# Down phase of an fp32 MLP kernel: four groups of products three uses apart instead of two, with later splits and loads at the phase edges

## What is computed

```python
h = h + rmsnorm(mix, post_mix_gain[l])
v = rmsnorm(h, pre_mlp_gain[l])
ff = jnp.square(jax.nn.relu(jnp.einsum("bsd,df->bsf", v, mlp_w_up[l].astype(v.dtype))))
ff = jnp.einsum("bsf,fd->bsd", ff, mlp_w_down[l].astype(v.dtype))
h = h + rmsnorm(ff, post_mlp_gain[l])
```

## Time and profile before

| | |
|---|---|
| median of 3 runs | 2196.18 us (2189.27 to 2198.07) |
| profiled execution, own time | 2191.95 us |
| its span, first to last instruction | 2188.8 us |
| TensorE busy | 97% |
| VectorE, ScalarE, GpSimd busy | 65%, 48%, 11% |
| mean granted TensorE clock | 0.992 of full speed |
| DMA, mean over the span | 182 GB/s |

### The profile page before, as it was taken

The page is one execution under the profiler, slowest core; times in us unless marked ns, Lnnn a source line. Parts: engine busy times, 40 slices in busy tenths (PEclk is TensorE's granted clock), DMA queues, the critical chain, the costliest instruction groups (busy, mean ns, idle before and its releaser), DMA issues.

```text
span 2188.8 us, 28875 instructions
## 1 busy us (share of the span) xinstructions
PE 2120.9 (97%) x9781; PEld 1743.9 (80%) x9781; DVE 1425.9 (65%) x2309; ACT 1049.8 (48%) x1821; POOL 237.0 (11%) x228
## 2 busy tenths in 40 slices
PE   8999999999999999989999899999899999999996
PEld 6777788888888788778888688888787888888885
DVE  4877666666666646776666766666576666666666
ACT  5564545555555534555555665555332333333333
POOL 6001000000001000033200000000333310000001
PEclk9999999999999999999999999999999999999999
DMA  7246644644544726578755865554877755444467
GB/s 262 109 152 207 205 154 135 201 146 145 196 150 144 259 87 199 154 232 275 254 152 151 272 178 145 144 142 130 308 240 242 264 187 163 135 154 135 143 151 168
DMA packets 317493, 397.82 MB, mean 182 GB/s; under 512 B 15296, under 2 KB 204256, under 8 KB 317392
## 3 DMA queue, kind: packets, MB, share of 16 engines
q1 hardware_dynamic: 295728, 317.46, 46.0%
q0 software_dynamic: 19360, 70.72, 10.3%
q10 hardware_dynamic: 2304, 8.39, 0.9%
HBM read 262.09 MB, written 134.41 MB: 181 GB/s over the span
## 4 chain that ended last, share of the span: by engine, by line
PE 81%; DVE 3%; DMA 2%; ACT 2%; issue 1%; SPq 0%; ACTq 0%; DVEq 0%; POOLq 0%
PE o_ps L1847 20%; PE o_ps L1849 19%; PE o_ps L1848 19%; PE m_unit_ps L516 18%; DMA o_s_lo<-ff_d 1%; PE o_ps L1878 1%; PE m_nd_ps L577 0%; PE m_bank L565 0%; PE m_nd_ps L576 0%; PE m_s_ps L556 0%; PE m_nd_ps L528 0%; PE m_nd_ps L529 0%; PE m_nd_ps L585 0%; DVE o_acc L2461 0%; DMA o_b_lo<-v_d 0%
## 5 line engine op out<-in xcount | busy, mean ns | idle before, releaser
L516 PE MATMUL m_unit_ps<-u_hi,w_hi 128*128 128x512 f32 x768 | 309.1, 402 | 1.4 <-ACT floor L796 1.1
L516 PE MATMUL m_unit_ps<-u_hi,w_lo 128*128 128x512 f32 x768 | 300.8, 392 | 0.0
L516 PE MATMUL m_unit_ps<-u_lo,w_hi 128*128 128x512 f32 x768 | 299.7, 390 | 0.0
L1847 PE MATMUL o_ps<-w_hi,o_s_hi 128*128 128x512 f32 x704 | 274.9, 391 | 7.0 <-ACT o_stage_c L2039 5.6
L1849 PE MATMUL o_ps<-w_hi,o_s_lo 128*128 128x512 f32 x704 | 274.0, 389 | 0.0
L1848 PE MATMUL o_ps<-w_lo,o_s_hi 128*128 128x512 f32 x704 | 273.9, 389 | 0.0
L2482 DVE TENSOR_TENSOR o_acc<-o_ps,o_acc 128x512 f32<-128x512 f32 x256 | 172.0, 687 | 148.8 <-PE o_ps L1849 148.7
L2071 ACT ACTIVATE o_s_hi<-o_s_lo 128x512 fp32r<-128x512 f32 x129 | 81.1, 631 | 270.7 <-DMA o_s_lo<-ff_d 270.2
L516 PEld LDWEIGHTS m_unit_ps<-u_hi,w_lo 128*128 128x128 f32 x768 | 144.5, 188 | 32.0
L516 PEld LDWEIGHTS m_unit_ps<-u_hi,w_hi 128*128 128x128 f32 x768 | 144.9, 189 | 29.7 <-issue 1.9
L516 PEld LDWEIGHTS m_unit_ps<-u_lo,w_hi 128*128 128x128 f32 x768 | 145.1, 189 | 27.6
(11 more groups left out here) (383 smaller groups left out, 4474.0 us busy)
## 6 DMA issues: line engine op xcount, KB each, us to landing
o_s_lo<-ff_d SPq DMA_DIRECT2D x129, 256.0 KB, 2.8
o_up_raw<-in_mlp_w_up SPq DMA_DIRECT2D x32, 1024.0 KB, 5.9
ff_d<-o_stage_c SPq DMA_DIRECT2D x128, 256.0 KB, 5.8
u_hi<-uhi_d SPq DMA_DIRECT2D x12, 2048.0 KB, 10.7
u_lo<-ulo_d SPq DMA_DIRECT2D x12, 2048.0 KB, 15.1
ff_d<-o_stage_s SPq DMA_DIRECT2D x96, 256.0 KB, 5.6
o_a_lo<-ff_d SPq DMA_DIRECT2D x95, 256.0 KB, 2.7
w_raw<-in_w_in POOLq DMA_DIRECT2D x24, 512.0 KB, 5.5
```

The lines of the kernel that those rows point to most:

```text
L516: last = nc.tensor.matmul(unit_bank[u][:], w[u][:, c, :], x[:, b, c, :], start=(c == 0 and z == 0), stop=(c == KT - 1 and z == 2))
L1847: nc.tensor.matmul(dst, sh, mh, start=(begins and i == 0), stop=False, skip_group_check=not begins)
```

## The change

Six edits. The groups of the down phase stand three uses apart, not two, so that the phase has 41 sets in place of 38 and the first sets hold only group 0 (three sets, six products), then groups 0 and 1. The idle slots s4 and a12 take products a11 and s2 of use 2, and s3 takes a12 of use 29. The split of each new form is placed no later than two steps ahead of its first use. The first chunk's forms are loaded later (at steps 0, 4, 7, 18 and not 0, 1, 3, 10), as are their splits, the stores of set 31 and the last gain vector. At the turn, form 2 is loaded ahead of the stores of set 14 and is split at the end of set 15, and forms 3 to 6 are split one place later each. GpSimd starts its slab sums when the left operands of set 3 are made, where it started when the first forms were.

```diff
-        sets = [[(p, s - 2 * DOWN[p][1]) for p in DOWN if 0 <= s - 2 * DOWN[p][1] < self.USES]
-                for s in range(self.USES + 6)]
+        sets = [[(p, s - 3 * DOWN[p][1]) for p in DOWN if 0 <= s - 3 * DOWN[p][1] < self.USES]
+                for s in range(self.USES + 9)]
...
-        other = {("a11", 1): "s3", ("s2", 1): "a22", ("a12", self.USES - 2): "a11", ("a12", self.USES - 1): "s2"}
+        other = {("a11", 1): "s3", ("s2", 1): "a22", ("a12", self.USES - 3): "s3", ("a12", self.USES - 2): "a11", ("a12", self.USES - 1): "s2"}
+        other |= {("a11", 2): "s4", ("s2", 2): "a12"}
...
-            self.low_at.append(-1 if m < 4 else max(min(self.high_at[m] + 2, m - 3), self.low_at[-1]))
+            self.low_at.append(-1 if m < 4 else max(min(self.high_at[m] + 2, m - 3), self.high_at[m], self.low_at[-1]))
...
-        rest = [(3, ("s4", 0)), (6, ("s3", 0)), (9, ("a22", 0)), (16, ("a12", 0))]
-        rest += [(self.index[p, 8 * c - 1] + 4, (p, c)) for c in range(1, 4) for p in DOWN]
+        rest = [(3, ("s4", 0)), (9, ("s3", 0)), (12, ("a22", 0)), (24, ("a12", 0))]
+        rest += [(min(self.index[p, 8 * c - 1] + 4, self.index[p, 8 * c] - 2), (p, c)) for c in range(1, 4) for p in DOWN]
...
# SP, up_set
+                if is_set(S, PAIRS - 1):
+                    load_form(2)
                 if not is_set(S, 0) and not is_set(S, SETS - 1):
                     store_ff(S - 1, 1 - b, 0 if is_set(S, PAIRS) else B)
                 if is_set(S, PAIRS - 1):
-                    for i in range(2, 7):
+                    for i in range(3, 7):
                         load_form(i)
...
# SP, down steps
-                if m in (0, 1, 3, 10):
-                    load_down({0: "s4", 1: "s3", 3: "a22", 10: "a12"}[m], 0)
-                if 5 <= m <= 8:
+                if m in (0, 4, 7, 18):
+                    load_down({0: "s4", 4: "s3", 7: "a22", 18: "a12"}[m], 0)
+                if 9 <= m <= 12:
...
# POOL
-            pool.wait_ge(*form_lo_made.at(14))
+            pool.wait_ge(*slot_lo_made.at(4 * 7))
...
# ScalarE, up_set (VectorE alike): turn is set 15, turned set 16
-                        second_form(4)
+                        second_form(3)
...
-                        second_form(5)
+                        second_form(4)
...
+                if turned:
+                    second_form(5)
...
-                if turn:
-                    second_form(2)
...
-                if turn:
-                    second_form(3)
...
+                if turn:
+                    second_form(2)
```

14 lines of the change are left out of this document (7 added, 7 removed).

## The result

| | before | after |
|---|---|---|
| median of 5 runs | 2194.13 us (2189.27 to 2198.07) | 2207.52 us (2204.70 to 2210.74) |
| profiled execution, own time and span | 2191.95, 2188.8 us | 2207.26, 2204.4 us |
| ratio | | 1.0075, 95% interval 1.0058 to 1.0093 |

The forecast was 2195.4 us (2183.5 to 2205.0), no measurable change, with a chance of 0.10 for slower. The median lies above that range.

A forecast was written before the change was run, and what follows sets the result against it. TensorE was taken as the bound, with only its pauses to win. Terms −3.8 − 3.4 + 0.3 + 1.0 + 1.6 + 1.5 + 2.0 = −0.8 gave 2191.15 us profiled; the median, 4.2 higher, 2195.4 (2183.5 to 2205).

The forecast's parts named there:

- the first steps: Start of the down phase: m = 5 waits for the copy of m = 4, pause about 6.5 us; +0.3 us.
- the tail: m = 214 to 221: operand loads have three products behind the one freeing their slot, before four; +2.0 us.
- GpSimd's start: Up phase: slab sums from set 3 remove TensorE's pauses in sets 1 and 2; −3.8 us, bounds −3.8 and 0.
- the turn: Sets 15 and 16: s4 of set 15 no longer waits for form 2, but a pause remains in set 16; −3.4 us.
- changes of a form: Three forms wanted one product earlier, at m = 30, 33 (+1.6 us) and 204 (+1.5 us).
- m = 7 to 30: Opening of the down phase: operand loads have four products behind the one freeing their slot, before six; +1.0 us.
- The slower rival: Opening and tail: operand loads land late and stall products, two pauses lower the clock; 2208 us, chance 0.12.
- three signs: Wrong if m = 5 starts within 3 us of its turn, set 16 has no pause, or opening landings average over 8 us.

The follow-up runs named there:

- later forms a step earlier: The changed kernel with each later form split at least three steps ahead of its first use, not two: 2199.49 us, 1.0040 of the kernel before.
- three repairs: The changed kernel with s4's first form split at step 4, s3's and a22's at 18 and 21, later forms three steps ahead: 2199.34 us, 1.0050 of before.

## Why the prediction was wrong

**Right: what bounds the kernel, the up phase, the first steps, the tail.** GpSimd's start and the turn were priced at −3.8 and −3.4 and gave −7.0 together, −2.8 and −4.1 in the pair of traces; each has a kernel of its own with a measured gain. That the sum came out this close is in part luck, since traces of one and the same up phase differ by almost 5 us in the start of m = 0. The first steps, +0.3, gave +0.4, with the wait where it was put. The tail, +2.0, gave +1.6.

**Wrong: the term "changes of a form", +1.6 and +1.5, which came to +7.1 and +6.5.** The prediction had the right places and the right wait, and named pauses of 1.4 to 3 us there; they were 2.4, 3.9 and 4.7. What it sized wrong was each pause.
- The chain. "Each is 2.72 − 1.3 = 1.4 late" took the quiet case's 6.67 us from an operand's load to the end of the form's split. It took 8.3 us for m = 30 (VectorE behind with other work) and 9.5 us for m = 33 (a split of 4.08 us beside GpSimd's additions for the 2.36 us that were taken for all, and a landing of 3.8). The allowance of 2.2 for a busier queue was too small for both.
- The raw form at m = 204. Its chain was counted from the operand alone, like the others. But a12 of chunk 3 has five products between its old values' last use and its first new one, two fewer than before, and the form landed only at 2123.6, 0.5 us before m = 204 should have started. That was to be read in the order. At most 1.8 us of the 4.66 are the operands that ScalarE took first (2123.6 to 2125.39).
- The clock. The sum counted a slow product behind the pause at m = 5, and none behind these three. After pauses of 2.42, 3.94 and 4.66 us the next product took 4.20, 4.41 and 4.41 us, 4.9 us over the stride in all. The earlier trace rows made this look safe: behind 2.60 us at m = 41 the next product came on time.

These sizes vary. In the five kernels that keep this order and these later splits, m = 30 starts 2.0 to 5.1 us over its stride and m = 33 1.1 to 4.7; m = 204 always 4.7 to 4.8. The last is the distance; the other two depend on when operands land and on whether the split falls beside GpSimd's additions.

What the experiments show of the cause: two apart, with all else changed, the same three forms (first used at m = 38, 41 and 196) start 2.2, 0 and 0 us over the stride. Three apart with the splits three steps ahead, m = 33 comes on time in both kernels that have it (later forms a step earlier, three repairs), m = 30 still waits, and m = 204 keeps 4 us. With seven products everywhere, m = 204's pause is gone, and in chunk 1 what is left follows GpSimd's additions (at m = 32 1.0 us over the stride in one kernel, 3.4 in the other, with the split at 2.36 and 4.51 us). So at m = 204 it is the distance, and at m = 30 and 33 mostly the split's step and length. How much the operands' extra product adds there, no kernel took apart.

**Wrong: the term "m = 7 to 30", +1.0, which came to +7.5 up to m = 18 alone.** The prediction named the split of s3 at step 9 ahead of the add that m = 12 waits for (m = 12 waited 1.2 us) but priced operand loads. The split of a22 at step 12 stands likewise ahead of the copy that m = 16 waits for, and it was left out: 3.78 us and 1.56 for the slow product. In the trace of before these two splits took 2.35 us each, and m = 7 to 18 lost 0.7 in all. The order has 12 products in sets of four now (m = 6 to 17), where the second product of a group follows two behind the first; it had 8.

**The slower rival gave the right time mostly for a wrong reason.** It put 2208 on operand loads that land late and stop the product that needs them, and 2207.5 was measured. TensorE waited for operands' low parts only 2.0 us in all (the line L2345 above), and landings of operands between 1549 and 1600 us had a median of 3.6 us, less than before (5.6). But a late operand does its harm another way: ScalarE takes it ahead of a form, so the form's split comes late. ScalarE sat idle for one 5.67 us before m = 16, 4.92 us before m = 33 and 6.45 us before m = 204, and two of these loads took 8.0 and 8.1 us to land. Outside the first steps no term priced a late operand on this path.

**The range** was too narrow at the top because the upper bounds of the form terms, +5 and +3, held no slow product and no slower split, and because I treated the terms' ends as independent: one mechanism, less time for a form, raised three of them together. None of the three signs that the prediction named for being wrong showed: they watched the first steps, the turn and the mean landing, and the loss was elsewhere.

The Trainium skill, "SBUF — State Buffer", section "🔬 SBUF: two separate sides", has GpSimd and a VectorE operation with two SBUF inputs exclude each other. The traces agree: a form split takes 2.36 us alone and 3.4 to 4.6 beside GpSimd's additions. I drew on it for the up phase, where TensorE gained from moving the additions all the same, and not for the form splits, where it cost time.

What stays open: which of the opening's loads, stores and splits frees m = 7 to 18, and what the operands' distance adds at the form changes of chunk 1.

## What to carry to other kernels

When an order is stretched, count for every shared buffer the products between its last old use and its first new one, at the edges too, where sets are smaller. A change of one or two there takes slack that the steady middle never shows. Count the steps from a split to its first use as well, and look at what stands ahead of it on its engine: a load of something else that lands late delays it too. Put a long operation of the engine that frees the accumulators where nothing waits behind it, and not between two products of one accumulator. Price each new pause with a slow restart as a chance, and each split at its length beside the engine that stretches it.

## What the runs showed of the hardware

Short pauses can cost clock too: behind a pause of 2.42 us the next product took 4.20 us in place of 2.72. It is not a matter of the pause's length alone: behind 2.60 us before the change the next product took 2.84 us (1675.44 − 1672.60). In a window with the end of the changed kernel's longest pause (7.83 us, to 1561.78) and the products behind it the granted clock was 0.75 of full speed on the mean, between its two levels of 1.2 and 2.4 GHz (0.5 and 1.0):

```profile
1560.00:1572.00 12.00, 10.22 (x36) 8.32 (x37) 7.91 (x12) 0.00 (x0) 2.78 (x3) 0.75 0.55 197
```
